# Four modulation blocks go in front of the experts' stage, and TensorE multiplies them between the router's steps

## The reference, cut to what matters

```python
def moe_swiglu(h, w_router, w1, w3, w2):
    logits = jnp.einsum("btd,de->bte", h, w_router).astype(jnp.float32)
    top_v, top_i = lax.top_k(logits, TOP_K)
...
mod = (cond @ w_mod[l] + b_mod[l])[:, None, :]
sh_a, sc_a, g_a, sh_f, sc_f, g_f = jnp.split(mod, N_MOD, axis=-1)
...
x = x + g_a * (jnp.concatenate([o_m, o_d], axis=-1) @ w_out[l])
```

## Time and profile before

| | us |
|---|---|
| median of 3 runs | 2095.27 |
| lowest, highest | 2092.81, 2095.79 |
| the profiled execution | 2093.15 |
| its span in the trace | 2091.3 |

### The profile page before, as it was taken

One profiled execution on the slowest core, in us unless ns is written; L12 is line 12 of the kernel. 1 busy time (PEld: TensorE's weight loads), 2 busy tenths in 40 slices (PEclk: granted clock), 3 DMA queues, 4 the chain that ended last, 5 costly groups with the idle time before them and its releaser, 6 DMA issues.

```text
span 2091.3 us, 28839 instructions
## 1 busy us (share of the span) xinstructions
PE 1990.1 (95%) x11776; PEld 1696.9 (81%) x11798; DVE 1672.5 (80%) x1753; ACT 1169.8 (56%) x1316; POOL 72.8 (3%) x121
## 2 busy tenths in 40 slices
PE   7999999999899999999999999898899999989999
PEld 6778899786678888887888888677689988869998
DVE  6778889887789898989889888878778887856444
ACT  3544434464677776777777777456444345654432
POOL 6001000000000000000000000000010000000000
PEclk8999999999999999999999999999899999999999
DMA  9855999645599999999999999824369994324552
GB/s 354 265 188 192 356 350 359 213 140 192 193 336 341 359 366 333 351 360 366 330 351 364 363 337 350 293 95 148 121 230 346 352 356 145 122 72 150 182 185 97
DMA packets 251211, 554.41 MB, mean 265 GB/s; under 512 B 10076, under 2 KB 75856, under 8 KB 251072
## 3 DMA queue, kind: packets, MB, share of 16 engines
q1 hardware_dynamic: 247252, 544.13, 73.7%
q0 software_dynamic: 3552, 8.29, 1.1%
q10 hardware_dynamic: 268, 0.07, 0.0%
HBM read 551.40 MB, written 1.05 MB: 264 GB/s over the span
## 4 chain that ended last, share of the span: by engine, by line
PE 71%; DVE 15%; ACT 7%; issue 4%; DMA 4%; SPq 0%; ACTq 0%; DVEq 0%
PE bank L511 21%; PE bank L513 21%; PE bank L512 21%; DVE ring_lo L1990 4%; ACT ring_hi L1293 3%; DVE acc L1930 2%; DMA ring<-in_ffn_w_dram 1%; PE bank L902 1%; PE bank L1110 1%; DVE work L2175 1%; DMA ring<-in_w_in_dram 1%; DMA ring<-in_ada_w_dram 1%; PE bank L539 1%; DMA ring<-in_w_gate_dram 1%; DVE st L2179 1%
## 5 line engine op out<-in xcount | busy, mean ns | idle before, releaser
L1990 DVE TENSOR_TENSOR ring_lo<-ring,ring_hi 128x2048 fp32r<-128x2048 f32 x417 | 949.2, 2285 | 251.6 <-ACT ring_hi L1293 248.9
L1293 ACT ACTIVATE ring_hi<-ring 128x2048 fp32r<-128x2048 f32 x417 | 794.8, 1912 | 473.7 <-PE bank L513 225.5
L511 PE MATMUL bank<-hh,ring_hi 128*128 128x256 f32 x1152 | 328.2, 285 | 9.8 <-DVE ring_lo L1990 8.0
L512 PE MATMUL bank<-hl,ring_hi 128*128 128x256 f32 x1152 | 326.1, 283 | 0.0
L513 PE MATMUL bank<-hh,ring_lo 128*128 128x256 f32 x1152 | 326.0, 283 | 0.0
L513 PE MATMUL bank<-ring_hi,hl 128*128 128x256 f32 (+2 forms) x768 | 236.0, 307 | 0.0
L511 PEld LDWEIGHTS bank<-hh,ring_hi 128*128 128x128 f32 x1152 | 220.9, 192 | 13.6 <-issue 7.0
L511 PE MATMUL bank<-ring_hi,hgh 128*128 128x512 f32 (+1 forms) x576 | 220.6, 383 | 7.4 <-DVE ring_lo L1990 3.0
L512 PEld LDWEIGHTS bank<-hl,ring_hi 128*128 128x128 f32 x1152 | 221.1, 192 | 0.9 <-issue 0.5
L513 PEld LDWEIGHTS bank<-hh,ring_lo 128*128 128x128 f32 x1152 | 221.0, 192 | 0.0
L511 PE MATMUL bank<-ring_hi,hh 128*128 128x256 f32 (+2 forms) x672 | 209.3, 311 | 11.8 <-DVE hl L2054 6.5
(11 more groups left out here) (427 smaller groups left out, 2815.2 us busy)
## 6 DMA issues: line engine op xcount, KB each, us to landing
ring<-in_moe_w_dram SPq DMA_DIRECT2D x264, 1024.0 KB, 5.3
ring<-in_ada_w_dram SPq DMA_DIRECT2D x48, 1024.0 KB, 7.4
ring<-in_w_mod_dram SPq DMA_DIRECT2D x48, 1024.0 KB, 7.6
ring<-in_w_in_dram SPq DMA_DIRECT2D x40, 1024.0 KB, 5.5
ring<-in_ffn_w_dram SPq DMA_DIRECT2D x33, 1024.0 KB, 5.7
ring<-in_w_gate_dram SPq DMA_DIRECT2D x22, 1024.0 KB, 5.1
ring<-in_w_up_dram SPq DMA_DIRECT2D x22, 1024.0 KB, 5.3
ring<-in_w_down_dram SPq DMA_DIRECT2D x22, 1024.0 KB, 5.1
```

The source lines that it names most:

```text
L511: pe.matmul(ps, xh, wh, start=first, stop=False)
L512: pe.matmul(ps, xh, wl, start=False, stop=False)
L1293: act.activation(ring_hi[i % NH][:, 0:z], ring[n % NS][:, 0:z], ACT.Copy).then_inc(*s.hi(("hi", home(s, i), i)))
L1990: dve.tensor_tensor(ring_lo[n % NS][:, 0:z], ring[n % NS][:, 0:z], hi, ALU.subtract).then_inc(*s.lo(("lo", home(s, i), i)))
```

## The change

The four blocks of (4, 2) go into the plan in front of the experts' first block, and join `ON_PE`. PE multiplies them with the replicated column of silu(c) as its stationary side, in float32, into the banks `Y[1]`: one half block after the transposes, two behind the router's products, one behind the (3, 2) sum, two behind `places`, two behind the gather, and then adds the bias with ones. ACT copies the two banks to `gate[1]` ahead of its flag. All 34 `turn_over` multiplications around the router are left out, and the experts' first use of `Y` waits for the copies.

```diff
-        ON_PE = [("mod", 0, 0, 0), ("mod", 0, 1, 0)] + [("mod", 0, 2, p) for p in range(4)]
+        ON_PE = [("mod", 0, 0, 0), ("mod", 0, 1, 0)] + [("mod", m, 2, p) for m in (0, 4) for p in range(4)]
...
-        put_blocks(weave(ffn_blocks(*[(("moe", x), a["moe_w1"][0, x], a["moe_w3"][0, x], a["moe_w2"][0, x]) for x in range(8)]), mods((4, 2)), 6, 6))
-        IN_MOE = [(4, 2)]
+        put_blocks(mods((4, 2)))
+        put_blocks(weave(ffn_blocks(*[(("moe", x), a["moe_w1"][0, x], a["moe_w3"][0, x], a["moe_w2"][0, x]) for x in range(8)]), [], 6, 6))
...
-                if (m, j) in IN_MOE:
-                    i, need = moe1 + 4, len(split)
+                if (m, j) == (4, 2):
+                    continue
...
+            def router_gate(p, k, bias=False):
+
+                key, ps = ("mod", 4, 2, p), Y[1]
+                w = ring[where[key] % NS][:, :].rearrange("p (k c) -> p k c", k=2)
+                pe.wait_ge(*at("arrived", where[key]))
+                for h in range(2):
+                    x = pe.matmul(ps[h][:, :], bc(csil[:, 8 + 2 * p + k:9 + 2 * p + k], [128, 128]), w[:, k, 512 * h:512 * h + 512],
+                                  start=p == 0 and k == 0, stop=False)
+                if k:
+                    x.then_inc(*main.prod(("mod used", 4, 2, p)))
+
+            def router_gate_sum():
+
+                pe.wait_ge(*at("bias", 4, 2))
+                for h in range(2):
+                    x = pe.matmul(Y[1][h][:, :], ones, acc_of(2)[:, 512 * h:512 * h + 512], start=False, stop=True)
+                    x.then_inc(*main.small(("gatesum", 4, h), ("sum", 4, 2)))
...
             def router():
+                pe.wait_ge(*at("r", 2, 1, 1))
+                router_gate(0, 0)
                 ps = psum("router")
...
                 x.then_inc(*main.small(("router",)))
+                router_gate(0, 1)
+                router_gate(1, 0)
                 ps = psum("router turned")
...
                 summed((3, "router"))
-                turn_over(Y[0][0][:, :], 6)
+                router_gate(1, 1)
                 ps = psum("places")
...
                 x.then_inc(*main.small(("places",)))
-                turn_over(Y[0][0][:, :], 12)
+                router_gate(2, 0)
+                router_gate(2, 1)
...
-            turn_over(Y[0][0][:, :], 8)
             router()
             gather_first(0)
             gather_first(1)
-            turn_over(Y[0][0][:, :], 8)
+            router_gate(3, 0)
+            router_gate(3, 1)
+            router_gate_sum()
...
+            def router_gate():
+
+                act.wait_ge(*at("r", 1, 1, 1))
+                for h in range(2):
+                    act.wait_ge(*at("gatesum", 4, h))
+                    act.activation(gate[1][:, 512 * h:512 * h + 512], Y[1][h][:, :], ACT.Copy).then_inc(*main.act(("gate", 4, h)))
...
             first_rows()
+            router_gate()
             act.wait_ge(*at("flag"))
```

More of the change, by code:

```diff
@@ L1074, in moe_all @@
             def moe_all():
-                y_free = {("moe", e): [("r", 2, t, h) if e == 0 else ("many", e - 1, "kept", t, h) for t in range(2) for h in range(2)] for e in range(8)}
+                y_free = {("moe", e): [("many", e - 1, "kept", t, h) for t in range(2) for h in range(2)] for e in range(1, 8)}
+                y_free["moe", 0] = [("r", 2, t, h) for t in range(2) for h in range(2)] + [("gate", 4, h) for h in range(2)]
                 swiglu(many, [("moe", e) for e in range(8)], 3, y_free)
@@ L1131, in down @@
                     if g == 0:
-                        for z in ([("few", "y", e - 2, h) for h in range(2)] if e >= 2 else [("r", 2, t, h) for t in range(2) for h in range(2)]):
+                        for z in ([("few", "y", e - 2, h) for h in range(2)] if e >= 2 else [("r", 2, t, h) for t in range(2) for h in range(2)] + [("gate", 4, h) for h in range(2)]):
                             pe.wait_ge(*at(*z))
```

## The result

The changed kernel takes 2112.82 us, median of four runs (2109.29 to 2114.37), against 2094.04 for the kernel before in the same session: a ratio of 1.0088, 95% interval 1.007 to 1.0106, slower. The forecast was 2111.7, within 2105 to 2119. The profiled execution of after took 2109.29 us, its span is 2107.5; the profiled one of before has a span of 2091.3. Unrounded the two differ by 16.1 us, and it is these 16.1 that the traces can explain; the medians differ by 18.8, and the other 2.6 lie in executions that weren't traced.

The account below looks back on a forecast made before the run. PE was taken to bound the experts' stage, a chain of small steps the router. Terms +14.8 +2.4 +7.4 -5.5 -1.7 = +17.4, on 2093.15 or 2095.27, gave 2110.6 or 2112.7; forecast 2111.7 us, range 2105 to 2119.

Parts of the forecast that it names:

- The wait: Ahead of the boundary after the mixer: ACT and DVE wait to split the experts' late first block; +14.8 us.
- The clock: Router's start: after PE's idle time its granted clock is at half for 6 us of resumed work; +2.4 us.
- The entrance: Router to the experts' stage: gate products and copies make ACT's first ring_hi there later; +7.4 us.
- transposes: Router's two transposes on PE, behind gate products (0,1) and (1,0): 2.68 us later.
- places: Router's `places` on PE, behind the (3,2) sums and gate product (1,1): at 532.85 in place of 529.74.
- gather: Gather on PE, behind gate products (2,0) and (2,1): starts at 537.53 in place of 533.85, +3.7 us.
- the row's own distance: ACT's branch into the experts' stage: first ring_hi 3.61 us behind its last operation ahead of the branch, as before.
- The experts' stage: DVE loses eight multiply-adds, so PE's pauses behind them go or shrink; -5.5 us.
- The first projection: Second model's first projection: the (4,2) sum leaves PE; -1.7 us, bounds 0 and -1.9.
- (1): Late block: its wait is not paid and the clock doesn't fall; +0.2, 2095.5 us, no change; 4%.
- (2): Experts' stage paced by transfers: four fewer blocks give -12.1 in place of -5.5, 2105.1 us; 7%.
- (3): Clock stays down through the router, priced at 6 to 14 us: 2116 to 2123; 9%.

Follow-up runs that it names:

- the wait alone: Kernel before with only the load order changed: the experts' first block loaded fifth instead of first, used as before, gate unmoved; 2112.87 us, ratio 1.0094.
- the change without it: Changed kernel with the splitting ahead stopped at the experts' first block, which is split later with the second one; 2096.21 us, ratio 1.0008.
- the narrowed kernel: Kernel before with DVE's eight multiply-adds of (4, 2) 8 columns wide instead of 1024, all loads kept; 2088.58 us, ratio 0.9979.

## Why the prediction was right

**The wait** (+14.8): measured +14.74, by the chain as put: load at 513.82, ring_hi at 519.01, ring_lo at 520.95, boundary at 523.16 (forecast 513.35, 518.6, 520.5, 522.75, to which the trace's offset of 0.5 comes). That it is the cause, and not only present, is shown by the wait alone (1.0094) and the change without it (1.0008).

**The clock** (+2.4, taken as 6 us at half speed behind 534.2): mis-sized. Measured +0.79, all of it behind the second XN (4.78 us to the router's first product for 3.99). The clock was back at full 3.4 us after the second transposes began at 534.58, not 6. In that time the second transposes took 1.97 where they had taken 1.09 (the 1.04 of the earlier trace rows, which the forecast used, is the first ones'), and the gate products 2.71, where four such records at full clock take 1.88:

```profile
519.34 1.09 PE L593 MATMUL bank<-cst,XN 128*128 128x128 f32 x8 [0.21 <-DVE XN L2017]
```
```profile
547.26 1.88 PE L554 MATMUL bank<-ring,csil 128*128 128x512 f32 x4
```

The 0.79 is about what the transposes lost; that the gate products' 0.83 lay beside the wait for hl fits this, but no run isolates it. The wait alone, with idle multiplications in that place, shows +0.87 for the same stretch. The bounds of 0 to 6.0 held it. The Trainium skill's "TensorE: Matmul & The Clock Gate", section "Terms", puts the penalty at half of a throttled stretch, by which an estimate for the 17 us of this trace is 8.5; the trace has 0.8, since PE had work in only 5.65 of them and waited on DVE for the rest.

**The entrance** (+7.4, bounds 5.3 to 9): measured +8.13. By its steps, against the router's first product: transposes +2.75 (forecast 2.68), places +3.20 (3.11), gather +3.64 (3.7), the second gate copy 23.96 behind the product, that is at 546.42 in the times of before (546.51). The step that failed is the last, "3.61, the row's own distance": it measured 4.41. I had taken the branch's gap as fixed, and it wasn't. The change also frees ring slots here, and one of their loads is under way while ACT branches; with it held back the distance was 3.32. I had listed these loads and booked them at nothing, for their own consumers only. The forecast took the longer gap into neither its sum nor a reason for a bound; that 9 held it is room left for something else.

**The experts' stage** (-5.5, bounds 0 to -10.4): measured -5.66, and -5.57 in the narrowed kernel, where nothing else is changed. There four pauses went whole. The second kept 1.22 where I had left about 1.0. Those are 5.1 us of pauses; the other 0.5 isn't traced.

**The first projection** (-1.7): -1.61 at the first operation behind it. The -0.75 further on, and the offset of +0.50, belong to no term; kernels that share this code differ there by as much.

**The rivals.** The wait was paid (1); transfers don't pace the stage (2); the clock did not stay down through the router (3): the window from 538 to 558 has 20.00 us of PE work at 1.00.

**What was luck.** The sum of the terms was +17.4; the traces have +16.4 for the same terms, because an oversized clock (1.6) and an undersized entrance (0.7) offset each other in part. The medians differ by 18.8. The forecast of 2111.7 lies within 1.1 us of the measured 2112.82 also because it was added up from a base of 2093.15 to 2095.27, where the session's median was 2094.04; runs of one kernel spread over 4 to 5 us.

**A version beside both.** With the wait cut and the copies on DVE the same move comes to 0.9988 to 0.999 of the kernel before in three measurements, some 2 us, with intervals that end at 0.9999 and 1.0: just clear of no change. The narrowed multiply-adds show what there was to win in the experts' stage, 0.9979. That PE's own time for the gate takes back half of it is what the traces suggest (PE begins the experts 4.7 us later, 23.36 for 18.69); it isn't shown by a run of its own.

## What to carry to other kernels

When blocks are put in front of others in a queue of loads, look first at who takes the displaced block earliest: a helper that prepares work ahead, on an engine that runs in order, turns a load that comes later by 35 us and is still in time for its product into a 15 us stop of everything queued behind the helper. Putting matrix work into the gaps of a chain pays only while gaps are left; past that its total counts, wherever it stands. And keep what waits for the last of that work off the engines that still have a branch to take.

## What the runs showed of the hardware

ACT's idle time behind the branch, booked as issue, goes with what the DMA engines do: 2.98 us before, 2.72 with the load held back, 3.82 with the load under way. Over the traces of this case it is 2.66 to 2.98 us in the six in which the DMA share of that gap is 0.03 to 0.05 and 3.52 to 4.13 in the five in which it is 0.49 to 0.65; the three with the copies on DVE (2.66, 2.67 and 5.27) have it booked to DVE's copy. The Trainium skill's "Runtime: NRT & Kernel Launch", section "Instruction fetch mechanics", says that a taken branch out of the loaded pages waits for a DMA fetch of its target. That fits a gap that grows with a transfer of 1 MB in flight, and the profile lists a few packets of an instruction queue in either window (6 and 4), though not for which engine. The Trainium skill's section gives no time for it, and that the fetch is what waits is argued here, not shown.

A clock at half for 17 us cost 0.8 us, and idle multiplications that took it to 3.4 us saved nothing: in both traces the half-speed time took in the second transposes and the first gate products, which is where PE's time counted. A second fall, of some 3 us behind PE's pause of 3.24, cost nothing, because PE's next wait for DVE took it up.
